# Loading x's first rows from ScalarE's queue instead of the sync engine's, in a two-layer sparse and differential attention trunk

## What is computed

```python
for i in range(DEPTH):
    h = _rmsnorm(x, pre_norm_g[i])
    z = h @ w_in[i]
    ...
    y = jnp.concatenate([oa * jax.nn.silu(ga), ob * jax.nn.silu(gb)], axis=-1) @ w_out[i]
    x = x + _rmsnorm(y, post_norm_g[i])
    gate = jax.nn.sigmoid(x @ w_ple_gate[i])
    e = (p[i] @ w_ple_proj[i]) * gate
    x = x + _rmsnorm(e, ple_norm_g[i])
```

## Time and profile before

| | |
|---|---|
| three executions | 359.46, 360.78 and 361.03 us; median 360.78 us |
| the profiled execution | 361.26 us, of which the span of its trace is 359.5 us |
| mean granted TensorE clock | 0.994 of full speed |
| TensorE busy | 350.3 us (97%) |
| weight loads into TensorE | 292.5 us (81%) |
| VectorE busy | 263.7 us (73%) |
| ScalarE busy | 227.6 us (63%) |
| GpSimd busy | 66.2 us (18%) |
| moved by the DMA engines | 61.12 MB, mean 170 GB/s |

### The profile page before, as it was taken

How to read it: one execution, slowest core, us unless ns; L and a number is a source line. 1 busy time by engine, 2 the same in 40 slices (tenths; PEclk the granted TensorE clock), 3 DMA queues, 4 the chain that set the end, 5 groups by cost and what they waited for, 6 DMA issues and landing times.

```text
span 359.5 us, 5682 instructions
## 1 busy us (share of the span) xinstructions
PE 350.3 (97%) x1925; PEld 292.5 (81%) x1925; DVE 263.7 (73%) x560; ACT 227.6 (63%) x459; POOL 66.2 (18%) x121
## 2 busy tenths in 40 slices
PE   6999999999999999999999999999999999999992
PEld 5898888888888888888888878888888888888882
DVE  2786879988955776786787577988895658678543
ACT  4897656686587854664677564787658686365221
POOL 1135353132200000003015524004230000000000
PEclk9999999999999999999999999999999999999997
DMA  7995378962654555558675936546455536550011
GB/s 254 380 355 187 117 230 112 323 183 85 182 172 124 169 177 175 177 162 140 220 204 154 334 102 209 169 119 177 116 144 162 165 121 231 163 168 22 0 46 72
DMA packets 31948, 61.12 MB, mean 170 GB/s; under 512 B 2376, under 2 KB 4688, under 8 KB 31920
## 3 DMA queue, kind: packets, MB, share of 16 engines
q1 hardware_dynamic: 30784, 57.48, 50.6%
q0 software_dynamic: 1120, 3.28, 5.1%
q10 hardware_dynamic: 16, 0.00, 0.0%
HBM read 59.71 MB, written 1.05 MB: 169 GB/s over the span
## 4 chain that ended last, share of the span: by engine, by line
PE 94%; issue 2%; DMA 1%; ACT 1%; DVE 0%; POOLq 0%; DVEq 0%; POOL 0%; SPq 0%
PE proj L1210 25%; PE proj L1212 25%; PE proj L1211 25%; PE sc L1293 3%; PE tr L1354 2%; PE sc L1144 2%; PE tr L1311 2%; PE pv L1375 2%; PE pv L1370 1%; DMA raw<-in_w_ple_proj_dram 1%; PE proj L1128 1%; PE proj L1155 1%; PE proj L1116 1%; PE proj L1144 1%; PE proj L1222 1%
## 5 line engine op out<-in xcount | busy, mean ns | idle before, releaser
L1210 PE MATMUL proj<-w_hi,act_hi 128*128 128x512 f32 (+1 forms) x392 | 157.5, 402 | 0.0
L1212 PE MATMUL proj<-w_hi,act_lo 128*128 128x512 f32 (+1 forms) x392 | 152.3, 389 | 0.0
L1211 PE MATMUL proj<-w_lo,act_hi 128*128 128x512 f32 (+1 forms) x392 | 151.8, 387 | 0.0
L817 DVE TENSOR_TENSOR w_lo<-raw,w_hi 128x1024 fp32r<-128x1024 f32 (+1 forms) x102 | 121.7, 1210 | 14.5 <-ACT w_hi L595 13.8
L595 ACT ACTIVATE w_hi<-raw 128x1024 fp32r<-128x1024 f32 (+2 forms) x103 | 103.0, 1026 | 5.0 <-DMA raw<-in_w_ple_proj_dram 1.8
L1212 PEld LDWEIGHTS proj<-w_hi,act_lo 128*128 128x128 f32 x392 | 73.6, 188 | 15.5
L1210 PEld LDWEIGHTS proj<-w_hi,act_hi 128*128 128x128 f32 x392 | 73.7, 188 | 14.6 <-issue 1.0
L1211 PEld LDWEIGHTS proj<-w_lo,act_hi 128*128 128x128 f32 x392 | 73.9, 189 | 12.8
L536 POOL TENSOR_TENSOR rstd<-var,minus_half 128x1 f32<-128x1 f32 x12 | 6.8, 564 | 184.5 <-DVE var L807 162.8
L718 ACT ACTIVATE probs<-probs,neg_max 128x128 f32<-128x128 f32 (+1 forms) x64 | 28.2, 444 | 6.0 <-DVE neg_max L960 6.0
L526 POOL TENSOR_TENSOR v_all<-work,rot_tab 128x128 f32<-128x128 f32 x16 | 9.6, 598 | 77.9 <-ACT work L595 77.8
(11 more groups left out here) (202 smaller groups left out, 438.2 us busy)
## 6 DMA issues: line engine op xcount, KB each, us to landing
raw<-in_w_in_dram SPq DMA_DIRECT2D x59, 512.0 KB, 4.3
raw<-in_w_out_dram SPq DMA_DIRECT2D x16, 512.0 KB, 3.7
raw<-in_w_ple_gate_dram SPq DMA_DIRECT2D x16, 512.0 KB, 3.8
raw<-in_w_in_dram SPq DMA_DIRECT2D x7, 324.0 KB, 5.8
raw<-in_w_ple_proj_dram SPq DMA_DIRECT2D x4, 512.0 KB, 4.2
resid<-in_x_dram SPq DMA_DIRECT2D x2, 512.0 KB, 7.9
probs<-in_w_in_dram SPq DMA_DIRECT2D x2, 512.0 KB, 9.3
g_ple<-in_ple_norm_g_dram POOLq DMA_DIRECT2D x2, 512.0 KB, 7.8
```

Of the source, the lines that this page charges most:

```text
L817: nc.vector.tensor_tensor(w_lo[:, g % SLOTS, 0:nk * cols], landing(g, nk * cols), w_hi[:, g % SLOTS, 0:nk * cols].bitcast(fp32), ALU.subtr ...
L1210: nc.tensor.matmul(ps, src_hi[:, b, k0 + k, :], hi, start=(first_u and k == 0), stop=False)
L1211: nc.tensor.matmul(ps, src_hi[:, b, k0 + k, :], lo, start=False, stop=False)
L1212: last = nc.tensor.matmul(ps, src_lo[:, b, k0 + k, :], hi, start=False, stop=last_k)
```

## The change

The load of x's block 0 leaves the sync engine's queue, where it stood between g1 and x's block 1, and is issued by ScalarE, behind its first copy and so behind its first table load. Block 1 stays where it was. Sizes, tiles, semaphores and everything that waits for them stay the same.

```diff
@@ block.sync
-            def load_x(b):
-                sp.dma_start(resid[:, b, :], x[0, b * P:(b + 1) * P, :]).then_inc(x_in[b], 16)
-
...
                 if g == 1:
-                    load_x(0)
-                    load_x(1)
+                    sp.dma_start(resid[:, 1, :], x[0, P:2 * P, :]).then_inc(x_in[1], 16)
@@ block.scalar
             act.dma_start(g8[:, :], pre_norm_g[0, :].rearrange("(k p) -> k p", p=P)).then_inc(g8_in, 16)
             act.wait_ge(const_done, 2)
             copy(lam_e[:, :], minus_half[:, 0:2])
+            act.dma_start(resid[:, 0, :], x[0, 0:P, :]).then_inc(x_in[0], 16)
```

## The result

The changed kernel takes 361.36 us (median of 22 executions, 360.17 to 362.41) against 360.47 us (22 executions, 358.95 to 361.52) of the kernel before: ratio 1.0027, interval 1.0016 to 1.0037. It is 0.9 us slower, a small but measurable loss. 361.3 us had been forecast. The number came out by luck: the whole way to it turned out to be another than the one forecast.

What follows compares the result with a forecast made beforehand. TensorE was taken to bound the kernel from h0 on. The g0 term gave +0.5 us and all others 0; on the median 360.78 us this made 361.3 us, range 359.9 to 362.9 us.

Steps and rivals of the forecast that it cites:

- the +0.5 us: Whole loss forecast, from a later g0 and h0: middle between 0.7 us and 0.35 us, range 0 to 1.5 us.
- What bounds the kernel: TensorE, 97% of the span, continuously busy from matmul step h0 at 6.97 us; x not on the chain of waits.
- The issue: ScalarE's issue at about 2.87 us, 0.47 to 0.61 us long, fits its idle time; sooner sync-queue issues gain nothing: 0.
- g0, +0.7 us: First weight unit lands later beside x's half, shifting ScalarE's copy and h0 by 0.7 us, between 0 and 1.35 us.
- 0.35 and 1.35 us: Delays of g0 by alternating packets: 0.35 us with 8 KB left per DMA engine, 1.35 us on a late one.
- g1, +0.9 us: Second weight unit lands about 0.9 us later, delaying x's norm; hidden before TensorE's transposes: cost 0, at most 0.2 us.
- The half of the clock: If the clock rises when it did, half of g0's 0.7 us delay, 0.35 us, reaches the end.
- The rule: Transfers issued by different engines interleave on the same 16 DMA engines, saving only sequencer time; speaks against a gain.
- The first ("hidden"): Rival: x's half fits into idle DMA share, g0 keeps its landing; 360.8 us, chance 0.35 together with the fourth.
- The second: Rival: the hole before h0 grows to 2.6 us and the clock rises much later; +3.2 us, 363.9 us, chance 0.13.
- The third: Rival: x's norm held TensorE, so earlier x gains 1.0 us, or 1.8 us with the clock: 359.0 us, chance 0.07.
- The fourth: Rival: ScalarE's issue waits for the tiny copy, x still ends behind g1; 360.8 us, chance 0.35 together with the first.

Runs made afterwards that it cites:

- the experiment with the square first: Changed kernel, with x's first half squared before g1's copy on ScalarE and its variance before g1's low part on VectorE: 361.49 us, ratio 1.0041 to the kernel before.
- new order: Kernel before, with x's first half issued between g0 and g1 on the sync engine and its steps ahead of g1's on every engine: 360.63 us, ratio 1.0011.
- both halves: Changed kernel, with both halves of x issued by ScalarE, one behind the other: 361.98 us, ratio 1.0052 to the kernel before.
- second half: Kernel before, with x's second half issued by ScalarE and the first left on the sync queue behind g1: 361.53 us, ratio 1.0045.
- sliver: Kernel before, with only 16 columns (8 KB) of x's first half issued by ScalarE, the rest on the sync queue behind g1: 360.22 us, ratio 1.0002.

## Why the prediction was right, and where it wasn't

*The number and the sign* came out: 361.3 us forecast, 361.36 us measured; slower by a little, within 0.5%. That is luck: the +0.5 us was put on g0, which cost nothing in either profile of the changed kernel, and g1 and x's norm, which had been put at nothing, carried the loss. (The lower end of the range, 359.9 us, comes to 360.0 us by its own rule, 360.8 - 0.8; nothing hangs on it.)

*What bounds the kernel.* "x isn't on this chain at all" was true of the profiled execution and false of the second, which has x's landing on the chain and 0.91 us of idle time behind it. The first could have warned: its 361.26 us is above all three executions then at hand, and a slack of some tenths was read from it.

*The issue.* That it costs ScalarE nothing was right. That it happens behind the table load was wrong: the issue is at 2.01 us, while the table load runs (until 2.67 us) and before the copy written ahead of it starts (2.68 us). It takes 0.37 us, less than the 0.47 to 0.61 us named. On the sync queue, w_in was not issued "up to 0.47 us sooner" but up to 1.5 us (the fourth unit at 4.54 us instead of 6.05 us). The time at which x's half starts to move, put at 4.0 us, has no row of its own in these views; that the half landed at 9.78 us, in the experiment with the square first, says that the sooner issue brought nothing.

*g0, +0.7 us.* Failed. g0's copy began at 5.41 us in both profiles of the changed kernel, the soonest that ScalarE can (it ends p's copy then). The chain's first transfer didn't grow, it left the chain. By its own test ("wrong if g0 lands sooner than 6.1 us") this step is wrong. Neither of the prices worked out for it, 0.35 and 1.35 us, was paid there. Before the change g0's copy began at 5.41 us in one profile and 6.20 us in the other, so its landing varies by itself. It was waited for in four of the experiments too, until 5.74 us (new order), 5.86 us (both halves), 5.94 us (second half) and 6.08 us (sliver). Whether x's half held it back in some of these, or does in executions of the changed kernel that have no profile, isn't shown.

*g1, +0.9 us.* Right in size for the first profile (+0.92 us; +1.88 us in the second, beyond the upper bound of 1.35 us). Right too was the way on: copy, low part of g1 in front of the variance, norm. Wrong was its price, 0 to 0.2 us. The norm's half was ready at 12.56 us and the transposes started at 13.67 us, which is 1.1 us of cover, of which the forecast had 0.3 us left; all of it was an accident of a late h0 and a low clock. In the second profile of before there is no cover, but a hole.

*The half of the clock.* "0.35 us if the clock rises when it did" has no part in the loss of these two executions: in both the clock was late (2.04 us for h0's four matmuls), and TensorE still stood idle for 0.27 and 0.64 us in front of the transposes. It does bear on the kernel before, where a late clock hides part of what the change costs.

*The rule.* That issuing from two engines gives no bandwidth, since all transfers interleave on the same DMA engines (the Trainium skill, DMA: Bandwidth & Descriptors, "Issuing engines are not separate DMA queues"), is what the rows show: x's half landed at 9.78 us against 9.79 us, and g1 paid. From 1 to 10 us the DMA engines moved 2.82 and 2.60 MB in the two profiles of the changed kernel, and 2.68 and 2.61 MB in those before.

*The rivals.* The first ("hidden") is out, 1.0016 being the lower end of the interval. The second happened nowhere in the changed kernel that a profile shows, but may be what goes with the large hole of the experiment that moved the issue back. The third took for granted that an x on the path would come sooner; x can be on the path, and wasn't sooner in the execution that shows its landing. The fourth expected no change of the time, and there is one.

*Open:* how many executions of each kernel are held by what, how the delay of g1 grows with the bytes beside it, why g1's landing differs by 0.94 us between two executions of one program, and why g0 is late in some.

## What to carry to other kernels

A transfer moved to another engine's queue isn't moved to another wire: look at what it now travels beside, and follow that transfer's landing through the in-order engines to the next wait. Before a wait is called covered, see where the cover comes from in a second execution, when what covers it depends on a landing or on the clock: here one profile had 1.1 us of cover and the next a hole of 0.91 us. A landmark on the bounding engine whose start plus a constant gives the time in every profile with the same order of work on that engine (here 347.6 us) turns a question of 0.3% into one of microseconds, which two or three profiles answer.

## What the runs showed of the hardware that was not expected

- A transfer written behind an activation in ScalarE's program was issued before that activation ran: at 2.01 us, with the copy ahead of it at 2.68 us; and at 4.93 us, with the copy ahead of it running from 4.92 to 5.52 us. Both issues came some 0.05 us behind the end of what the wait in front of the activation asks for: GpSimd's constants (1.82 + 0.14 = 1.96 us) and TensorE's transposes of p (3.77 + 1.11 = 4.88 us).
- The same load (x's first half), issued 0.2 us sooner on a queue of its own, landed at 9.78 us against 9.79 us; issued at 4.93 us it took 6.6 us to land, with w_in units issued ahead of it by the sync engine.
- One program's g1 landed at 9.42 us in one execution and at 10.36 us in another, while before the change it was 8.50 and 8.48 us.
- The four matmuls of h0 took 2.04 us (1.2 GHz) or 1.17 us (2.4 GHz for the most part) in two executions of the same kernel, the clock having risen in front of them or behind. This is read from the pace; the granted clock printed for these stretches is 1.00 in both.
